# A dense expert layer whose second product keeps its sums in PSUM, tokens in rows, the second table streamed past loaded weights

## The chip, the cores and the metric

One core of one Trainium2 chip runs the whole program. The metric is the device time of one execution in microseconds (us); the median of three timed runs stands for a kernel.

## What is computed

Two transformer blocks follow each other on 512 tokens of 1024 values, in 32-bit floats. The change touches the end of the second block, a layer of 16384 small experts of which each token uses 8 times 16, and the final norm:

```python
q = (hc @ w_query).reshape(TOKEN_CHUNK, PEER_HEADS, 2, PEER_HALF)
...
gate = jax.nn.softmax(top_s, axis=-1)
u = expert_u[expert_idx]
act = jax.nn.gelu(jnp.einsum('thkd,td->thk', u, hc).astype(jnp.float32), approximate=False)
vv = expert_v[expert_idx]
return jnp.einsum('thk,thkd->td', (gate * act).astype(hc.dtype), vv)
...
x = x + peer_ffn(h2, ...)
return rmsnorm_2(x, final_g)
```

## The kernel before

Most tokens are computed densely. The first DT = 416 tokens are multiplied with all of both tables, in 128 tiles of 128 experts each. For a tile of the first table (a **U part**) the sum over the 1024 values of h gives one number per expert and token; GELU and the gate (zero for experts that the token did not choose) turn it into a weight; a tile of the second table (a **V part**) is multiplied with these weights and added to x. The other 96 tokens (3 sets of 32) go **by rows**: GpSimd gathers, for 32 tokens and four groups of experts at a time, 128 table rows (512 KB), and DVE reduces them against h (first 96 steps, line 1710) or adds them up with their weights (last 96 steps, lines 1720 and 1723), one step per gather.

A 32-bit product is made of three on TensorE: every operand is split into a high part and a remainder, and `mm3` multiplies high by high, high by remainder and remainder by high. The tables arrive as raw tiles of 512 KB (`stream`, slots of a ring of 4: SP loads `raw`, ACT makes `hi`, POOL makes `lo` on line 600). h is `inH`, `inL`; weights are `WH`, `WL`. x is kept transposed, as `xT`: 8 pieces k of 128 values, tokens along the row.

In a **U part** the table is the loaded operand and 416 tokens are streamed: 8 values of k by three products, 24 products. In a **V part** the table is the loaded operand too, and 416 columns of weights are streamed: for each of the 8 pieces k of x a pair of tiles gives 6 products in bank k mod 4, and DVE adds that bank to `xT` (`add`, line 1701). TensorE waits (`y_added`) until the bank is free again. A pair of tiles so has 48 products in its V parts and 8 additions on DVE.

The order is written out per engine. 48 U parts are computed before the loop: 20 while DVE looks for the chosen experts, 24 between the batches in which DVE builds the gates as one-hot products (`onehots`, 52 batches of 8 tokens, lines 1666 to 1670), and 4 behind them; 16 of their results are spilled to memory. The expert loop goes by pairs: 8 pairs with V parts alone (`HEAD`), 40 with U parts 32 tiles ahead and V parts, 16 with V parts alone. On ACT each pair has the copies of the stored results (line 1017), the high parts of the weights (1022) and of the tables (1041, 1108), and the GELU (1052); on DVE the gating (1692), the remainders (1697), the additions and the steps of the rows. For each set TensorE turns h (`turn_h`) and later the sums of the set (`turn_acc`). At the end the final norm needs all of x: squares, a sum over partitions on TensorE, a root, and the scaling of 8 pieces (1783) with one output transfer each.

## Time and profile before

| what | us |
| --- | --- |
| median of 3 timed runs | 2474.28 (2474.09 to 2475.71) |
| the profiled execution, its own time | 2468.48 |
| its span in the profile | 2466.7 |
| first product of the expert loop starts | 1496.80 |
| last product of the expert loop starts | 2453.59 |

The profile is a page with busy time by engine, by slices and by groups of instructions, and a trace that can be asked for a stretch. PE is TensorE's products, PEld its weight loads, DVE, ACT and POOL the other engines, SP issues transfers. A product's record is longer than the distance to the next one, because products overlap: the distance of two starts is what a product costs.

### The profile page before, as it was taken

The numbers are of one execution on the slowest core, as the hardware profiler recorded it, in microseconds if no ns is written. First come the engines' busy times: TensorE is split into PE (matmuls) and PEld (weight loads), VectorE is DVE, ScalarE is ACT, GpSimd is POOL, SyncE is SP. The second block draws the span as 40 slices with busy tenths as digits, with TensorE's granted clock in tenths as the row PEclk, the third lists the DMA queues.
The fourth block names the chain that finished last, engine by engine and source line by source line (L and its number), as shares of the span: only waits on it lengthen the run. The fifth ranks groups of instructions, "written<-read, shape, count | busy, mean of one in ns | idle before, by whom it ended". The sixth has DMA issues, their size and how long they took to land.

```text
span 2466.7 us, 37389 instructions
## 1 busy us (share of the span) xinstructions
PE 2404.9 (97%) x13120; PEld 2160.3 (88%) x13120; DVE 1685.8 (68%) x3413; ACT 929.9 (38%) x1473; POOL 1329.5 (54%) x1183
## 2 busy tenths in 40 slices
PE   7999999999999999999998999999999999999998
PEld 6785788888888886778998899899999999999998
DVE  6476733332499977779999985866766667575566
ACT  3146122222322346514354554333333343434443
POOL 5520565656555662364410006777777777776553
PEclk9999999999999999999999999999999999999999
DMA  4210233223232222132225678978888888786453
GB/s 171 94 52 27 77 102 102 94 100 105 85 111 94 95 85 82 49 105 86 90 90 185 249 267 277 344 257 279 266 276 270 270 277 272 256 299 208 144 169 100
DMA packets 211993, 404.48 MB, mean 164 GB/s; under 512 B 118432, under 2 KB 124960, under 8 KB 208544
## 3 DMA queue, kind: packets, MB, share of 16 engines
q1 hardware_dynamic: 64224, 233.36, 28.8%
q0 software_dynamic: 27648, 100.68, 10.9%
q10 hardware_dynamic: 120000, 68.89, 9.4%
q8 instruction: 69, 1.13, 0.2%
q14 instruction: 52, 0.43, 0.1%
HBM read 370.10 MB, written 32.77 MB: 163 GB/s over the span
## 4 chain that ended last, share of the span: by engine, by line
PE 72%; DVE 19%; issue 4%; POOL 3%; ACT 1%; DMA 0%; ACTq 0%; DVEq 0%; POOLq 0%; SPq 0%
PE bank L1790 22%; PE bank L1792 22%; PE bank L1791 22%; POOL lo L600 3%; DVE ohg L1670 2%; DVE lo L1609 2%; DVE oh L1666 1%; PE bank L1948 1%; DVE oh L1667 1%; PE bank L1959 1%; PE bank L1935 1%; DVE rows L1710 1%; DVE idx L1568 1%; DVE idx L1560 1%; DVE scb L1561 1%
## 5 line engine op out<-in xcount | busy, mean ns | idle before, releaser
L600 POOL TENSOR_TENSOR lo<-raw,hi 128x256 fp32r<-128x256 f32 (+1 forms) x948 | 1131.0, 1223 | 994.3 <-ACT hi L686 559.9
L1790 PE MATMUL bank<-inH,hi 128*128 128x512 f32 (+1 forms) x2112 | 790.5, 374 | 18.0 <-DVE inL L1137 13.4
L1792 PE MATMUL bank<-inH,lo 128*128 128x512 f32 (+1 forms) x2112 | 781.7, 370 | 0.0
L1791 PE MATMUL bank<-inL,hi 128*128 128x512 f32 (+1 forms) x2112 | 781.5, 370 | 0.0
L1790 PEld LDWEIGHTS bank<-inH,hi 128*128 128x128 f32 x2112 | 396.7, 188 | 67.2 <-POOL lo L600 12.8
L1792 PEld LDWEIGHTS bank<-inH,lo 128*128 128x128 f32 x2112 | 396.6, 188 | 43.5
L1791 PEld LDWEIGHTS bank<-inL,hi 128*128 128x128 f32 x2112 | 397.2, 188 | 42.0 <-issue 0.2
L1701 DVE TENSOR_TENSOR xT<-xT,bank 128x416 f32<-128x416 f32 x504 | 286.7, 583 | 213.3 <-PE bank L1792 108.5
L686 ACT ACTIVATE hi<-raw 128x1024 fp32r<-128x1024 f32 x236 | 247.9, 1056 | 405.0 <-PE bank L1792 392.2
L1790 PE MATMUL bank<-WH,hi 128*128 128x416 f32 x1024 | 358.9, 350 | 8.0 <-DVE xT L1701 7.2
L1791 PE MATMUL bank<-WL,hi 128*128 128x416 f32 x1024 | 357.7, 349 | 0.0
L1792 PE MATMUL bank<-WH,lo 128*128 128x416 f32 x1024 | 357.4, 349 | 0.0
L1041 ACT ACTIVATE hi<-raw 128x1024 fp32r<-128x1024 f32 x176 | 179.8, 1047 | 208.0 <-PE bank L1792 199.7
L1790 PEld LDWEIGHTS bank<-WH,hi 128*128 128x128 f32 x1024 | 192.5, 188 | 11.0 <-DVE xT L1701 9.0
L1792 PEld LDWEIGHTS bank<-WH,lo 128*128 128x128 f32 x1024 | 192.7, 188 | 0.3
L1791 PEld LDWEIGHTS bank<-WL,hi 128*128 128x128 f32 x1024 | 192.6, 188 | 0.3
L1692 DVE TENSOR_TENSOR bank<-bank,Gd 128x416 f32<-128x416 f32 x128 | 76.0, 595 | 114.1 <-ACT bank L1017 97.2
L1487 DVE SCALAR_TENSOR_TENSOR bank<-u,gn,bank 128x512 f32<-128x512 f32 x224 | 148.2, 750 | 0.0
L1723 DVE SCALAR_TENSOR_TENSOR bank<-rows,gate_sp,bank 128x1024 f32<-128x1024 f32 x93 | 119.4, 1284 | 1.3
L1710 DVE CUSTOM_DVE_ANT_0 rows<-bank,rows 128x1024 f32<-128x1024 f32 x96 | 116.0, 1218 | 0.0
L1052 ACT ACTIVATE A<-bank 128x416 f32<-128x416 f32 x80 | 41.5, 519 | 193.7 <-PE bank L1792 191.2
L1022 ACT ACTIVATE WH<-bank 128x416 fp32r<-128x416 f32 x128 | 65.6, 513 | 120.5 <-DVE bank L1692 98.1
(325 smaller groups left out, 2920.8 us busy)
## 6 DMA issues: line engine op xcount, KB each, us to landing
raw<-stream SPq DMA_DIRECT2D x440, 512.0 KB
Gd<-gates ACTq DMA_DIRECT2D x32, 832.0 KB
gates<-stage_a ACTq DMA_DIRECT2D x13, 1024.0 KB, 4.8
gates<-stage_b ACTq DMA_DIRECT2D x13, 1024.0 KB, 4.1
A<-spilled ACTq DMA_DIRECT2D x8, 416.0 KB
tbl<-gqa ACTq DMA_DIRECT2D x8, 384.0 KB, 3.2
xT<-x SPq DMA_DIRECT2D x4, 512.0 KB, 7.8
out<-xT ACTq DMA_DIRECT2D x8, 256.0 KB, 2.0
```

The lines of the kernel that those rows point to most:

```text
L600: ins = pool.tensor_tensor(lo[:, r, part], raw[:, r, part], hi[:, r, part].bitcast(F32), ALU.subtract)
L686: act.activation(hi[:, r % RING, :], raw[:, r % RING, :], ACT.Copy).then_inc(hi_done, 1)
L1022: act.activation(WH[:, j % 2, e, :DT], staged(j, e), ACT.Copy).then_inc(high_w, 1)
L1041: act.activation(hi[:, r, :], raw[:, r, :], ACT.Copy).then_inc(hi_done, 1)
L1487: done.append(chain.mark(dve.scalar_tensor_tensor(to, *tap(j), d, ALU.mult, ALU.add)))
L1692: dve.tensor_tensor(a, a, Gd[:, buf, :, 2 * (j % 2) + e, :], ALU.mult).then_inc(gate_done, 1)
L1701: dve.tensor_tensor(xT[:, k, :DT], xT[:, k, :DT], B[k % 4][:, :DT], ALU.add).then_inc(y_added, 1)
L1710: dve.tensor_tensor_reduce(out=rows[r][:, :], in0=held, in1=rows[r][:, :], scale=1.0, scalar=0.0, op0=ALU.mult, op1=ALU.add, accum_out=dot ...
L1723: dve.scalar_tensor_tensor(held, rows[r][:, :], weight, held, ALU.mult, ALU.add).then_inc(row_used, 1)
L1790: pe.matmul(bank, wh, xh, start=start, stop=False)
L1791: pe.matmul(bank, wh, xl, start=False, stop=False)
L1792: return pe.matmul(bank, wl, xh, start=False, stop=stop_)
```

## The change

- 128 tokens go by rows instead of 96 (4 sets), so DT is 384 (three blocks of 128); 256 steps and gathers instead of 192. h for them is turned once, before the loop, and copied into four groups by transfers on ACT's queue (`spread_h`).
- In a V part the **weights** are the loaded operand and the table is streamed: for each block of 128 tokens three products by two halves of 512 columns, 18 products in all. They add to six PSUM banks (three blocks by 1024 values) over all 128 tiles; x is turned into those banks first (`turn_x`), and there is no addition on DVE and no `y_added`.
- The loop goes by single tiles: 47 with a V part alone, then 80 turns of a U part (tile t+1) and a V part (tile t), then the last V part. Weights have 4 buffers.
- The remainders of the tables are made by POOL for odd slots and by DVE for even ones.
- One more U part (21) comes ahead of the batches and one fewer (23) between them; there are 48 batches instead of 52.
- The steps are dealt out by `steps_of`: a tile with a V part alone counts 3, another 8. Gathers are issued one tile ahead, into 6 buffers.
- The final norm goes by token: ACT squares a block's 1024 values and adds them up, DVE scales (`scale_block`); the output is stored by blocks, the rows' block ahead of the loop's end.

```diff
-SET, SETS = 32, 3
+SET, SETS = 32, 4
 DT = T - SET * SETS
+DB = DT // P
 GROUPS = P // SET
-PHASE_PAIRS = (5, 5, 5, 5, 4, 4, 4)
-FIRST_PAIR = 4
-ROWS_AHEAD = 5
+ROWS_AHEAD = 6
...
-EARLY = 19
+EARLY = 20
...
+FIRST_STEPS, LAST_STEPS = 4, 122
+PHASES = ((FIRST_STEPS, 75), (78, LAST_STEPS))
...
+def v_slot(t):
+    return t if t < V_ONLY else min(V_ONLY + 2 * (t - V_ONLY) + 1, N_REST - 1)
...
+    return sum(3 if at < V_ONLY else 8 for at in range(first, t + 1))
...
+def steps_of(t):
+    for phase, (first, last) in enumerate(PHASES):
+        if first <= t <= last:
+            n, whole = N_STEPS // 2, share(first, last)
+            return range(phase * n + n * share(first, t - 1) // whole, phase * n + n * share(first, t) // whole)
...
+            with sp.Fori(1, N_REST // RING) as i:
+                for r in range(RING):
+                    sp.wait_ge((lo_even, lo_odd)[r % 2], i * 2 + (r // 2 - 1))
+                    load(i * RING + (S_REST + r), r)
...
+            def odd_low(i):
...
+                if i % 2 == 0:
+                    return
+                n, r = S_REST + i, i % RING
+                pool.wait_ge(hi_done, n + 1)
+                pool.tensor_tensor(lo[:, r, :], raw[:, r, :], hi[:, r, :].bitcast(F32), ALU.subtract).then_inc(lo_odd, 1)
...
+            for t in range(NKEY):
+                if t + 3 <= V_ONLY:
+                    odd_low(t + 3)
+                elif V_ONLY <= t + 1 and t + 3 < NKEY:
+                    odd_low(u_slot(t + 3))
...
+                for g in steps_of(t + 1):
+                    gather(g)
...
+            def high_rest(i):
+                if i < N_REST:
+                    act.wait_ge(loaded[i % RING], 16 * ((S_REST + i) // RING + 1))
+                    act.activation(hi[:, i % RING, :], raw[:, i % RING, :], ACT.Copy).then_inc(hi_done, 1)
...
+            def spread_h(of):
...
+                act.wait_ge(row_used, SET * (of - 1)) if of >= 2 else act.wait_ge(x_turned, TT)
+                act.wait_ge(h_out, 2)
+                for grp in range(GROUPS):
+                    act.dma_start(h_rep[of % 2][grp * SET:(grp + 1) * SET, :],
+                                  h_tok[of * SET:(of + 1) * SET, :]).then_inc(h_in[of % 2], 16)
...
+            for t in range(NKEY - 1):
...
+                if t + 1 < N_EARLY:
+                    if t:
+                        move(t + 1)
+                else:
+                    act.wait_ge(slot_used, S_PEER + t + 2)
+                    act.activation(staged(t + 1), staged(t + 1), ACT.Gelu).then_inc(a_moved, 1)
+                    high_rest(u_slot(t + 1) + RING)
+                if t:
+                    high_w_part(t + 1)
...
+                act.wait_ge(y_done, t + 1)
+                high_rest(v_slot(t) + RING)
+                sparse_out(t)
+            for b in range(DB):
+                act.wait_ge(block_done, b + 1)
+                block_out(b, banks[:, 2 * b:2 * b + 2, :].rearrange("p b t -> p (b t)"), b + 1)
...
-            def add(j, k):
-                dve.wait_ge(y_done, j * KD + (k + 1))
-                dve.tensor_tensor(xT[:, k, :DT], xT[:, k, :DT], B[k % 4][:, :DT], ALU.add).then_inc(y_added, 1)
...
+            def even_low(i):
...
+                if i % 2:
+                    return
+                n, r = S_REST + i, i % RING
+                dve.wait_ge(hi_done, n + 1)
+                dve.tensor_tensor(lo[:, r, :], raw[:, r, :], hi[:, r, :].bitcast(F32), ALU.subtract).then_inc(lo_even, 1)
...
+                if of < SETS:
...
+                        dve.wait_ge(h_in[of % 2], 16 * GROUPS * (of // 2 + 1))
...
+            for t in range(NKEY - 1):
+                steps = list(steps_of(t))
+                if t + 3 <= V_ONLY:
+                    even_low(t + 3)
+                elif V_ONLY <= t + 1 < NKEY - 1:
+                    even_low(v_slot(t + 1))
+                for g in steps[:len(steps) // 2]:
                     step(g)
-                if j == V_PAIRS:
-                    fold_in(SETS - 1)
-            for e in (0, 1):
...
+                if t:
+                    gated(t + 1)
+                    low_part(t + 1)
+                for g in steps[len(steps) // 2:]:
+                    step(g)
...
+            dve.wait_ge(gain_in, 16)
+            scale_block(TT - 1, lambda half: x_sp[:, half * T:(half + 1) * T], 0)
+            for b in range(DB):
+                scale_block(b, lambda half: B[2 * b + half][:, :], b + 1)
...
+            def turn_x(b, at):
...
+                for k in range(KD):
+                    m = pe.matmul(B[at + k // 4][:, k % 4 * P:(k % 4 + 1) * P], xT[:, k, b * P:(b + 1) * P], ident, start=k % 4 == 0, stop=k % 4 == 3 and b == TT - 1)
+                m.then_inc(x_turned, 1)
...
-            def mix(j, wpar, n_lo, r):
...
-                pe.wait_ge(lo_done, n_lo)
-                pe.wait_ge(w_done, j * 2 + 2)
+            def expert_u(t, i, e, r):
+                pe.wait_ge(w_done, t - 1)
+                pe.wait_ge((lo_even, lo_odd)[r % 2], i)
                 for k in range(KD):
-                    if not isinstance(j, int) or j * KD + k - 3 > 0:
-                        pe.wait_ge(y_added, j * KD + (k - 3))
                     c = slice(k * P, (k + 1) * P)
-                    for e in (0, 1):
-                        m = mm3(B[k % 4][:, :DT], hi[:, r + e, c], lo[:, r + e, c], WH[:, wpar, e, :DT], WL[:, wpar, e, :DT],
-                                e == 0, e == 1)
+                    m = mm3(B[6 + e][:, :DT], hi[:, r, c], lo[:, r, c], inH[:, k, :DT], inL[:, k, :DT], k == 0, k == KD - 1)
+                m.then_inc(slot_used, 1)
+            def expert_v(t, i, w, r, stop=False):
+                pe.wait_ge(w_done, t + 1)
+                pe.wait_ge((lo_even, lo_odd)[r % 2], i)
+                for b in range(DB):
+                    tok = slice(b * P, (b + 1) * P)
+                    for x, table in ((WH, hi), (WH, lo), (WL, hi)):
+                        for half in (0, 1):
+                            last = x is WL
+                            m = pe.matmul(B[2 * b + half], x[:, w, tok], table[:, r, half * T:(half + 1) * T], start=False, stop=stop and last)
+                    if stop:
+                        m.then_inc(block_done, 1)
+                if not stop:
                     m.then_inc(y_done, 1)
...
+            pe.wait_ge(w_done, 2)
+            turn_x(0, 0)
+            with pe.Fori(0, V_ONLY // 4) as i:
+                for c in range(4):
+                    expert_v(i * 4 + c, i * 2 + (c // 2 + 1), c, c)
+            for t in range(V_ONLY // 4 * 4, V_ONLY):
+                expert_v(t, t // 2 + 1, t % W_TILES, t % RING)
+            with pe.Fori(0, (NKEY - N_EARLY) // 4) as i:
+                for c in range(4):
+                    t, at = V_ONLY + c, V_ONLY + 2 * c
+                    expert_u(i * 4 + (t + 1), i * 4 + (at // 2 + 1), (t + 1) % 2, at % RING)
+                    expert_v(i * 4 + t, i * 4 + ((at + 1) // 2 + 1), t % W_TILES, (at + 1) % RING)
+            expert_v(NKEY - 1, (N_REST - 1) // 2 + 1, (NKEY - 1) % W_TILES, (N_REST - 1) % RING, stop=True)
```

On TensorE, in the joint part of the loop, before: the end of a U part and the start of a V part (WH and WL are streamed, hi and lo loaded; `bank` is a PSUM bank).

```order
L1792 MATMUL bank<-inH,lo 128x416
L1790 MATMUL bank<-WH,hi 128x416 [waits y_added,w_done,lo_done]
L1791 MATMUL bank<-WL,hi 128x416
L1792 MATMUL bank<-WH,lo 128x416
L1790 MATMUL bank<-WH,hi 128x416
L1791 MATMUL bank<-WL,hi 128x416
L1792 MATMUL bank<-WH,lo 128x416
L1790 MATMUL bank<-WH,hi 128x416 [waits y_added]
```

And now: the end of a V part and the start of the next U part; rows with x2 are two products.

```order
L2373 REGISTER_ALU [waits w_done]
L2379 MATMUL bank<-hi,WH 128x512 [waits lo_even]
L2379 MATMUL bank<-hi,WH 128x512
L2379 MATMUL bank<-lo,WH 128x512 x2
L2379 MATMUL bank<-hi,WL 128x512 x2
L2379 MATMUL bank<-hi,WH 128x512 x2
L2379 MATMUL bank<-lo,WH 128x512 x2
L2379 MATMUL bank<-hi,WL 128x512 x2
L2379 MATMUL bank<-hi,WH 128x512 x2
L2379 MATMUL bank<-lo,WH 128x512 x2
L2379 MATMUL bank<-hi,WL 128x512 x2
L1840 MATMUL bank<-inH,hi 128x384 [waits lo_odd,w_done]
```

The table is now what is streamed, in 512 columns, two products for each loaded block, and nothing waits for an addition.

On DVE, in the first part of the loop (V parts alone), before: one pair with the first of its five steps (L1710).

```order
L1692 TENSOR_TENSOR bank<-bank,Gd 128x416 [waits a_moved,g_loaded0]
L1701 TENSOR_TENSOR xT<-xT,bank 128x416 [waits y_done] x2
L1697 TENSOR_TENSOR WL<-bank,WH 128x416 [waits high_w]
L1692 TENSOR_TENSOR bank<-bank,Gd 128x416 [waits a_moved,g_loaded0]
L1701 TENSOR_TENSOR xT<-xT,bank 128x416 [waits y_done] x2
L1697 TENSOR_TENSOR WL<-bank,WH 128x416 [waits high_w]
L1701 TENSOR_TENSOR xT<-xT,bank 128x416 [waits y_done]
L1710 ISA rows_126,dots<-bank,rows_126 128x1024 [waits h_turned,row_in0]
L1710 ISA dots 128x1
L1701 TENSOR_TENSOR xT<-xT,bank 128x416 [waits y_done]
L1710 ISA rows_127,dots<-bank,rows_127 128x1024 [waits row_in1]
L1710 ISA dots 128x1
```

And now: the weights of tiles 6 and 7 and the start of tile 8 (L1784 is a step, L1775 the remainder of a table tile).

```order
L1775 TENSOR_TENSOR lo<-raw,hi 128x1024 [waits hi_done]
L1762 TENSOR_TENSOR bank<-bank,Gd 128x384 [waits a_moved,g_loaded1]
L1767 TENSOR_TENSOR WL<-bank,WH 128x384 [waits high_w]
L1784 ISA rows_130,dots<-h_rep_136,rows_130 128x1024 [waits row_in1]
L1784 ISA dots 128x1
L1762 TENSOR_TENSOR bank<-bank,Gd 128x384 [waits a_moved,g_loaded1]
L1767 TENSOR_TENSOR WL<-bank,WH 128x384 [waits high_w]
L1784 ISA rows_134,dots<-h_rep_136,rows_134 128x1024 [waits row_in2]
L1784 ISA dots 128x1
L1775 TENSOR_TENSOR lo<-raw,hi 128x1024 [waits hi_done]
L1762 TENSOR_TENSOR bank<-bank,Gd 128x384 [waits a_moved,g_loaded0]
L1767 TENSOR_TENSOR WL<-bank,WH 128x384 [waits high_w]
```

The additions are gone; each second tile has a remainder that stands ahead of the gating, and one step follows each tile's weights.

On POOL, in the first part of the loop, before: the five gathers for a pair behind two remainders.

```order
L600 TENSOR_TENSOR lo<-raw,hi 128x1024 [waits hi_done] x2
L655 DMA rows_126<-rows_u,expert 128x1024 [waits row_used]
L655 DMA rows_127<-rows_u,expert 128x1024 [waits row_used]
L655 DMA rows_128<-rows_u,expert 128x1024 [waits row_used]
L655 DMA rows_129<-rows_u,expert 128x1024 [waits row_used]
L655 DMA rows_131<-rows_u,expert 128x1024 [waits row_used]
L600 TENSOR_TENSOR lo<-raw,hi 128x1024 [waits hi_done] x2
```

And now, one remainder and the gathers of two tiles in turn.

```order
L715 TENSOR_TENSOR lo<-raw,hi 128x1024 [waits hi_done]
L706 DMA rows_139<-rows_u,expert 128x1024
L706 DMA rows_129<-rows_u,expert 128x1024 [waits row_used]
L715 TENSOR_TENSOR lo<-raw,hi 128x1024 [waits hi_done]
L706 DMA rows_130<-rows_u,expert 128x1024 [waits row_used]
L706 DMA rows_134<-rows_u,expert 128x1024 [waits row_used]
L715 TENSOR_TENSOR lo<-raw,hi 128x1024 [waits hi_done]
L706 DMA rows_135<-rows_u,expert 128x1024 [waits row_used]
L706 DMA rows_138<-rows_u,expert 128x1024 [waits row_used]
```

A gather was issued a pair ahead of its use, behind the remainders of the pair before; it is now issued one tile ahead.

## Rows read from the trace of the kernel before

**Rows 1.** The page, section 1: busy time of each engine, share of the span, instructions.
```profile
PE 2404.9 (97%) x13120; PEld 2160.3 (88%) x13120; DVE 1685.8 (68%) x3413; ACT 929.9 (38%) x1473; POOL 1329.5 (54%) x1183
```

**Rows 2.** Stretches of the expert loop: busy time of each engine, clock, DMA.
```profile
core 0: us, PE busy (x) PEld busy (x) DVE busy (x) ACT busy (x) POOL busy (x), PEclk, DMA share, GB/s
1545.00:1580.00 35.00, 29.94 (x142) 27.84 (x141) 35.00 (x67) 11.78 (x18) 28.63 (x22) 0.93 1.03 384
1590.00:2300.00 710.00, 710.00 (x3836) 709.78 (x3835) 457.93 (x717) 275.93 (x399) 533.71 (x325) 1.00 0.79 263
```

**Rows 3.** Timeline, PE: start, duration; end of a V part, start of a U part.
```profile
2200.92 0.35 PE L1792 MATMUL bank<-WH,lo 128*128 128x416 f32 x1
2201.11 0.35 PE L1790 MATMUL bank<-inH,hi 128*128 128x416 f32 x1
2201.30 0.35 PE L1791 MATMUL bank<-inL,hi 128*128 128x416 f32 x1
```

**Rows 4.** Timeline, PE, 512 columns: the first and the last of eleven.
```profile
699.73 0.39 PE L1791 MATMUL bank<-inL,hi 128*128 128x512 f32 x1
...
701.99 0.39 PE L1792 MATMUL bank<-inH,lo 128*128 128x512 f32 x1
```

**Rows 5.** Timeline, PEld, 256 columns: the first and the last of seven weight loads.
```profile
122.51 0.19 PEld L1791 LDWEIGHTS bank<-lo,inH 128*128 128x128 f32 x1
...
123.22 0.19 PEld L1791 LDWEIGHTS bank<-lo,inH 128*128 128x128 f32 x1
```

**Rows 6.** Timeline, ACT: the first GELU of two pairs that follow each other.
```profile
1662.83 0.52 ACT L1052 ACTIVATE A<-bank 128x416 f32<-128x416 f32 x1 [2.47 <-PE bank L1792]
...
1680.75 0.52 ACT L1052 ACTIVATE A<-bank 128x416 f32<-128x416 f32 x1 [2.47 <-PE bank L1792]
```

**Rows 7.** Timeline, PE: the first and the last product of the expert loop.
```profile
1496.80 0.43 PE L1790 MATMUL bank<-WH,hi 128*128 128x416 f32 x1 [0.16 <-DVE WL L1697]
...
2453.59 0.34 PE L1792 MATMUL bank<-WH,lo 128*128 128x416 f32 x1
```

**Rows 8.** Groups by shape: busy us, mean ns, then idle before it.
```profile
L600 POOL TENSOR_TENSOR lo<-raw,hi 128x1024 fp32r<-128x1024 f32 x228 | 548.5, 2428 | 492.2 <-DVEq L1672 222.0 <-ACT hi L1041 153.4 <-ACT hi L1108 58.3
...
L1701 DVE TENSOR_TENSOR xT<-xT,bank 128x416 f32<-128x416 f32 x504 | 286.7, 583 | 213.3 <-PE bank L1792 108.5 <-issue 104.0
...
L1710 DVE CUSTOM_DVE_ANT_0 rows<-bank,rows 128x1024 f32<-128x1024 f32 x96 | 116.0, 1218 | 0.0
L655 POOL DMA_INDIRECT rows<-rows_u,expert x96 | 91.4, 952 | 30.8 <-issue 22.9 <-DVE dots L1710 6.4
...
L1609 DVE TENSOR_TENSOR lo<-raw,hi 128x1024 fp32r<-128x1024 f32 x32 | 39.2, 1225 | 5.5 <-DVE ohg L1670 5.1
```

**Rows 9.** Timeline, ACT, pairs with V work alone: one turn.
```profile
2321.48 0.94 ACT L1017 ACTIVATE bank<-A 128x416 f32<-128x416 f32 x2
2322.72 0.52 ACT L1022 ACTIVATE WH<-bank 128x416 fp32r<-128x416 f32 x1 [0.30 <-DVE bank L1692]
```

**Rows 10.** Timeline, POOL and DVE: the fifth gather and the step that uses it.
```profile
1528.65 0.94 POOL L655 DMA_INDIRECT rows<-rows_u,expert  x1 [0.30 <-issue]
...
1540.29 1.22 DVE L1710 CUSTOM_DVE_ANT_0 rows<-bank,rows 128x1024 f32<-128x1024 f32 x1
```

**Rows 11.** The page, section 6: issue to landing in us (last number).
```profile
tbl<-gqa ACTq DMA_DIRECT2D x8, 384.0 KB, 3.2
xT<-x SPq DMA_DIRECT2D x4, 512.0 KB, 7.8
```

**Rows 12.** Timeline, DVE, building of gates: the start of two batches.
```profile
1334.81 0.69 DVE L1666 TENSOR_TENSOR oh<-i1T,iota 128x1024 f16<-128x1024 f16 x1
...
1337.44 0.69 DVE L1666 TENSOR_TENSOR oh<-i1T,iota 128x1024 f16<-128x1024 f16 x1
```

**Rows 13.** Timeline, PE: half of one turn of 128 by 1024 values.
```profile
1525.75 1.05 PE L2318 MATMUL bank<-cs,res 128*128 128x128 f32 x8
```

**Rows 14.** Timeline, DVE: the last eight operations.
```profile
2458.87 5.35 DVE L1783 SCALAR_TENSOR_TENSOR xT<-xT,gn,bank 128x512 f32<-128x512 f32 x8 [1.25 <-PE bank L1879]
```

478 lines of the change are left out of this document (200 added, 278 removed).

## Prediction

> **What bounds the kernel now.** I first read the busy times: PE is busy for 97% of the span, DVE for 68%, POOL for 54% [rows 1]. PE's share counts records that overlap, so I went on to distances of starts. In the expert loop, between 1590 and 2300 us, PE is busy for all of the 710 us and DVE for 458 [rows 2], and a pair of tiles takes 1680.75 - 1662.83 = 17.92 us [rows 6]. A pair has 96 products, so one costs 17.92 / 96 = 0.1867 us, which is what neighbouring starts show (0.19, the bank changing between the first two without a gap) [rows 3]. The loop is bound by the number and width of products, and by nothing else there. From first to last product it takes 2453.9 - 1496.8 = 957.1 us [rows 7]. The products alone would need 24 pairs x 8.96 + 40 x 17.92 = 931.8 us; the other 25 are turns, waits near the start, where DVE is busy without a pause (35.00 of 35 us) and a moment at half clock (0.93 in those 35 us) [rows 2].
>
> **What a product costs at the new widths.** Ten distances at 512 columns take 701.99 - 699.73 = 2.26 us, 0.226 each [rows 4]. At 256 columns six take 123.22 - 122.51 = 0.71 us, 0.118 each [rows 5]. Between 256 and 416 columns the slope is 0.00043 us a column, between 416 and 512 it is 0.00041: a straight line. For 384 columns it gives 0.1867 - 32 x 0.00043 = 0.173 us. A U part goes from 24 x 0.1867 = 4.48 to 24 x 0.173 = 4.15 us, a V part from 4.48 to 18 x 0.226 = 4.07 us.
>
> The weight loads are busy for 709.78 of 710 us in the loop [rows 2], each 0.19 us long, as long as the distance of two products. At 256 columns they are still 0.19 long and start 0.118 apart [rows 5], so one load can run into the next, and I take the straight line. The Trainium skill (Perfetto Trace Analysis, Identifying the Most-Contended Engine) tells to judge the headroom of TensorE by the busy share of weight loads; by that this loop has none, and a narrower stream would bring nothing. That is rival B.
>
> **The loop, if PE is never held up:** 47 x 4.07 + 80 x (4.15 + 4.07) + 4.07 = 853.0 us, 104.1 less than now.
>
> **What the other engines need per turn.** In a joint turn of 8.22 us DVE has a gating and a remainder of weights (each like the 0.58 us of line 1701, an operation of that size), a table remainder of 1.225, and 128 / 45 = 2.84 steps of 1.22: 5.9 us. POOL has one remainder of 2.43 and 2.84 gathers, each 0.95 and about 0.3 between: 6.0 us [rows 8]. The additions that fell away were 8 x 0.58 us a pair on DVE. Both fit. The weights of tile t+1 have from the end of their U part until the next V part but one, 8.2 us, for a chain of less than 4. I expect no wait there.
>
> With V parts alone a turn is only 4.07 us, and three things show. (a) **The start:** ACT has two sets of h to send out, 8 issues of about 0.4 us, ahead of tile 2's weights: 4 us once (an estimate). (b) **The chain through ACT and DVE.** After a V part ends, ACT makes the high part of a table tile (1.0), DVE for each second tile its remainder (1.15 before it is free again), then gating 0.56, high weights 0.5, remainder of weights 0.56, with 0.1 to 0.3 us at each hand-over [rows 8, 9]. Sum about 4.35 us against 4.07: 0.3 us for each second tile, 22 x 0.3 = 7 us. Without the remainder the chain takes 3.6 and is hidden. (c) **The gathers.** A gather is now issued one tile ahead. From the end of V part t-1: 1.2 us to ACT's high part, 2.5 for POOL's remainder, then the gather at +3.9; it lands L later; the step takes 1.2, the next weights 1.9; V part t+3 is due at +12.2. There is room for L = 5.2 us. Every us above that delays one V part in four, about 10 us over the 42 tiles. L itself no row shows: before, a gather was issued 1540.29 - 1528.65 = 11.6 us ahead of its use and DVE never waited [rows 10]. The nearest rows are two other transfers, 3.2 us for 384 KB in a quiet place and 7.8 for 512 KB in a crowd [rows 11]. I take 6, somewhat above the middle, because the memory queues are full here: 8 us. The ends are 0 and 26. Together 4 + 7 + 8 = 19 us, and I keep 2.5 us for half clock (35 x 0.07), since PE again has small pauses: 874.5 us, **82.6 less**.
>
> **Ahead of the loop.** The building of gates is set by DVE: a batch takes 1337.44 - 1334.81 = 2.63 us [rows 12], 4 fewer batches save 10.5. The extra small copies for the fourth set I leave out. PE's narrower U parts save nothing there as DVE is later. `turn_h` and the turns of x between the batches lie in PE's slack (23 x 4.15 us of U parts is 12 less than 24 x 4.48); the last turn comes after the first weights: half a turn is 0.9 to 1.05 us [rows 13], so 1.8. DVE's first weights go one tile after the other, 0.5 more. Net **8.2 less**. If the weights are not what comes last here, it is between 4 and 10.
>
> **The end.** From the last product to the end of the span there are 2466.7 - 2453.9 = 12.8 us now; the last scaling ends at 2458.87 + 5.35 = 2464.2, 2.5 us before the end [rows 14]. After the change three blocks follow each other at 1.36 us; ACT needs about 1.6 for each (a pass over 1024 values like the 1.04 of the table's high part, and a root), DVE 1.6 (two scalings of 0.67, a reciprocal): ACT ends 2.1 us after the last product, DVE 2.6 later, and 2.5 for the store: 7.2. **5.6 less**, with the rows' block stored earlier. An end of 5 or 10 us is possible.
>
> **Sum:** 82.6 + 8.2 + 5.6 = 96.4 us less. The profiled span is 2466.7, its own time 2468.48; the median of the runs is 5.8 us above that, and I take the difference from the median: 2474.28 - 96.4 = 2378 us.
>
> **Rivals.**
>
> A. *The gathers are late.* For it: DMA demand in the first part is (2.06 x 0.524 + 0.197) MB in 4.07 us, 314 GB/s, and 361 while the spilled results come back; the trace shows 384 over 35 us at a share of 1.03 [rows 2]. So the queues stand full, and 7.8 us or more per gather is no wonder. With 7.8 the time is 18 us more, 2396; with 10 us 2418; I take 2407. Against: as the loop slows the demand falls.
>
> B. *Weight loads bind U parts.* Their 24 loads of 0.187 keep 4.48 us: 128 x 0.33 = 42 us lost, 2420. Rows 5 speak against it.
>
> C. *DMA can't feed the joint turns, and the kernel is slower.* A turn needs (4.84 x 0.524 + 0.197) = 2.73 MB in 8.22 us, 333 GB/s, for 80 turns. Before it was 263 GB/s at a busy share of 0.79 [rows 2]; 263 / 0.79 is 333, so if a byte keeps its cost there is nothing to spare. Against: the 384 GB/s. If the flow stops at 280 GB/s, a turn takes 9.76, 80 x 1.54 = 123 us more: 2501. It ends slower than before below about 291 GB/s (a turn of 9.4 us).
>
> D. *The accumulation costs more than the sum says.* Each product now goes to another bank than the last one; before the bank changed each 6 products in a V part, without a gap [rows 3]. If each of the 2304 cost 0.05 us more, it would be 115 us: 2493, slower. From 0.042 it eats the gain.
>
> **Chances.** The forecast 0.60, A 0.16, B 0.06, C 0.07, D 0.03; 0.08 for what I have not seen (0.04 of it for a larger gain, with no wait in the first part and a shorter end, 0.02 for no change, 0.02 for slower). The range from 2355 (no waits at all in the loop, a shorter end) to 2425 (the ends of the gathers' price, and B) holds the forecast, nearly all of A, and B. A measurement of this kernel can tell 0.2% from no change, some 5 us: faster 0.86, same 0.02, slower 0.12.
>
> **What would show it.** Starts of 384-column products 0.173 apart and of 512-column ones 0.226; U parts of the joint turns 8.22 us apart, with PE busy throughout and no wait named. In the first part, PE's waits on the remainder of weights, of a few tenths each second tile, and some on DVE steps that wait for their rows; first part near 210 us instead of 191. The loop should start about 8 us earlier, near 1488, and the end should take 7 us. If the turns are longer with DVE or POOL waiting for transfers, C is right; if PE is busy but the starts are further apart, B or D.

## The result, and the profile after

| | before | after |
| --- | --- | --- |
| median of the timed runs, us | 2474.72 (2474.09 to 2475.71) | 2448.03 (2441.85 to 2453.88) |
| ratio, 95% interval | | 0.9891 (0.9864 to 0.9919) |
| span of the profiled execution | 2466.7 | 2442.9 |
| first product of the loop | 1496.80 | 1491.85 |
| loop, first to last product | 957.1 | 945.1 |
| from there to the end of the span | 12.8 | 6.0 |

The kernel is faster by 26.7 us, 1.1%. The forecast was 96 us, and the time lies outside its range. The spans of the profiled executions differ by 23.8 us where 96.4 were forecast; of the missing 72.6 us, 70.6 are in the loop (945.1 for 874.5).

Section 1 of the page after, which answers [rows 1]: every engine but DVE has less to do.

```profile
PE 2342.1 (96%) x12272; PEld 1990.8 (81%) x12272; DVE 1734.1 (71%) x3084; ACT 872.5 (36%) x1386; POOL 1269.1 (52%) x1143
```

Stretches of the loop after, which answer [rows 2]. The first goes to the start of the 48th V part (46 turns with a V part alone and one joint turn), the second to the end; "first part" and "joint part" mean these two below, the joint part without the last V part of 4.1 us.

```profile
core 0: us, PE busy (x) PEld busy (x) DVE busy (x) ACT busy (x) POOL busy (x), PEclk, DMA share, GB/s
1491.85:1747.77 255.92, 218.54 (x874) 172.09 (x872) 145.91 (x207) 89.84 (x140) 129.81 (x72) 0.93 0.77 249
1747.77:2436.90 689.13, 674.42 (x3355) 605.92 (x3354) 556.86 (x543) 232.12 (x328) 488.81 (x288) 0.99 0.87 305
```

Without waits the forecast had 46 x 4.07 + 8.22 = 195.4 us for the first part; it took 255.9, at a granted clock of 0.93. The joint part has 79 x 8.22 + 4.07 = 653.4 against 685.0. What PE waited for, in the first part and after it (us in sum, times, longest):

```profile
PE bank L2379 <- DVE WL L1767: 37.3, 13, 5.2
...
PE bank L2379 <- DVE WL L1767: 13.7, 12, 5.2
```

The products themselves cost what was forecast, as the timeline of PE shows in the joint part, a U part between two V parts (it answers [rows 3, 4]; "x2" is two products):

```profile
1950.28 0.62 PE L2379 MATMUL bank<-hi,WL 128*128 128x512 f32 x2
1950.74 0.33 PE L1840 MATMUL bank<-inH,hi 128*128 128x384 f32 x1
...
1954.92 0.63 PE L2379 MATMUL bank<-hi,WH 128*128 128x512 f32 x2
...
1959.04 0.33 PE L1840 MATMUL bank<-inH,hi 128*128 128x384 f32 x1
```

The U part takes 1954.92 - 1950.74 = 4.18 us (forecast 4.15), the V part 4.12 (4.07). A turn is 8.30 to 8.31 instead of 8.22.

The groups by shape on DVE and POOL from 1485 on (busy us, mean ns, idle before and what ended it), which answer [rows 8]:

```profile
L1775 DVE TENSOR_TENSOR lo<-raw,hi 128x1024 fp32r<-128x1024 f32 x104 | 192.7, 1854 | 33.2 <-ACT hi L1120 33.0
L1795 DVE SCALAR_TENSOR_TENSOR acc<-rows,gate_sp,acc 128x1024 f32<-128x1024 f32 x124 | 192.6, 1553 | 29.7 <-DMA rows<-rows_v,expert 25.8 <-issue 0.3 <-DVE acc L1795 0.2
L1784 DVE CUSTOM_DVE_ANT_0 rows<-h_rep,rows 128x1024 f32<-128x1024 f32 x128 | 192.3, 1515 | 56.3 <-DMA rows<-rows_u,expert 54.7 <-issue 1.2
...
L715 POOL TENSOR_TENSOR lo<-raw,hi 128x1024 fp32r<-128x1024 f32 x104 | 284.1, 2732 | 259.7 <-ACT hi L1120 248.6 <-ACT hi L749 10.7 <-issue 0.2
L706 POOL DMA_INDIRECT rows<-rows_u,expert x128 | 172.2, 1345 | 32.3 <-issue 26.0 <-DVE dots L1784 1.8
```

DVE's steps, alone 1.22 us as in [rows 8], have a mean of 1.51 and 1.55; its remainder of a table tile, 1.225 before, has 1.85. POOL's remainder went from 2.43 to 2.73, its gather from 0.95 to 1.35. And DVE waits for its rows, 85 us in sum, which it never did before.

The timeline round one wait in the first part, POOL, then DVE, then PE:

```profile
1617.07 2.41 POOL L715 TENSOR_TENSOR lo<-raw,hi 128x1024 fp32r<-128x1024 f32 x1 [5.76 <-ACT hi L1120]
1619.62 1.77 POOL L706 DMA_INDIRECT rows<-rows_u,expert  x1
...
1625.49 2.39 POOL L715 TENSOR_TENSOR lo<-raw,hi 128x1024 fp32r<-128x1024 f32 x1 [2.09 <-ACT hi L1120]
...
1626.07 2.90 DVE L1784 CUSTOM_DVE_ANT_0 rows<-h_rep,rows 128x1024 f32<-128x1024 f32 x1 [1.88 <-DMA rows<-rows_u,expert]
...
1630.01 0.56 DVE L1767 TENSOR_TENSOR WL<-bank,WH 128x384 fp32r<-128x384 f32 x1 [0.56 <-ACT WH L1096]
...
1628.08 0.61 PE L2379 MATMUL bank<-hi,WL 128*128 128x512 f32 x2
1630.62 0.82 PE L2379 MATMUL bank<-hi,WH 128*128 128x512 f32 x2 [1.93 <-DVE WL L1767]
1631.24 1.05 PE L2379 MATMUL bank<-lo,WH 128*128 128x512 f32 x2
```

It reads from the top. POOL makes a remainder and issues the gather at 1619.62. DVE has waited 1.88 us for those rows when its step starts at 1626.07, 6.45 us after the issue. POOL has begun its next remainder at 1625.49, which ends at 1627.88; the step ends 1.09 us behind that, so it takes 2.90 instead of 1.22. The gating and the weights follow, and PE has waited 1.93 us. Then the products are slow for some 3 us: two cost 0.86 us (1631.24 on), at a granted clock of 0.50, that is 1.2 GHz, where 0.45 is usual. From 1551 us on PE waits like this about every 20 us, in every fourth or fifth turn.

The 1.09 us are no accident. In this trace 91 operations of DVE with two operands in SBUF (steps and table remainders) began while POOL was inside a remainder. Each of them ended 1.08 to 1.13 us behind the end of that POOL instruction, whenever it had begun, and so took 1.28 to 3.43 us; the 185 that met no remainder took 1.21 to 1.33. It goes the other way too: 69 remainders of POOL began inside such an operation of DVE, and all ended 2.23 to 2.26 us behind its end. And all 107 gathers that took more than 1.3 us on POOL ended 0.81 to 0.84 us behind such an operation of DVE. So the two engines don't share at a lower speed; the one that comes second does nothing until the other's instruction is over.

The timeline of ACT shows a third thing: two places where issues of transfers hold it for 10 us. In the first the first of the four issues takes 8.11 us and the others 0.61 each; the second is one issue.

```profile
1811.92 0.37 ACTq L1078 DMA_DIRECT2D Gd<-gates  x1
1812.47 10.05 ACTq L1127 DMA_DIRECT2D h_rep<-h_tok  x4
...
2121.81 0.37 ACTq L1078 DMA_DIRECT2D Gd<-gates  x1
2122.30 9.56 ACTq L1154 DMA_DIRECT2D gain_row<-last_gain  x1
```

Behind them stand the longest turns of the joint part: 10.88 and 12.03, 13.71 and 11.26 us.

### The profile page after: what moved, and what is told of

It is laid out like the page before. It is cut to its first block, busy times and chain, and to the rows that moved or that the text cites. A ratio compares the mean times of both kernels' runs of the same rounds, so it can differ in the third digit from the quotient of the medians.

```text
span 2442.9 us, 34890 instructions
## 1 busy us (share of the span) xinstructions
PE 2342.1 (96%) x12272; PEld 1990.8 (81%) x12272; DVE 1734.1 (71%) x3084; ACT 872.5 (36%) x1386; POOL 1269.1 (52%) x1143
## 4 chain that ended last, share of the span: by engine, by line
PE 54%; DVE 19%; issue 8%; DMA 8%; POOL 7%; ACT 3%; ACTq 1%; DVEq 0%; POOLq 0%; SPq 0%
PE bank L1840 13%; PE bank L1842 13%; PE bank L1841 13%; PE bank L2379 9%; DMA rows<-rows_u,expert 4%; DMA rows<-rows_v,expert 3%; POOL lo L651 3%; POOL lo L715 3%; DVE acc L1795 3%; DVE ohg L1740 2%; ACT hi L1120 1%; PE bank L1998 1%; DVE lo L1679 1%; PE bank L2009 1%; PE bank L1985 1%
## 5 line engine op out<-in xcount | busy, mean ns | idle before, releaser
L651 POOL TENSOR_TENSOR lo<-raw,hi 128x256 fp32r<-128x256 f32 (+1 forms) x740 | 631.7, 885 | 770.4 <-ACT hi L749 551.8
L1840 PEld LDWEIGHTS bank<-inH,hi 128*128 128x128 f32 x2112 | 398.4, 189 | 80.8 <-issue 16.7
L715 POOL TENSOR_TENSOR lo<-raw,hi 128x1024 fp32r<-128x1024 f32 x104 | 284.1, 2732 | 259.7 <-ACT hi L1120 248.6
L2379 PE MATMUL bank<-hi,WH 128*128 128x512 f32 x768 | 251.1, 409 | 52.1 <-DVE WL L1767 51.0
L2379 PE MATMUL bank<-lo,WH 128*128 128x512 f32 x768 | 245.3, 401 | 0.0
L2379 PE MATMUL bank<-hi,WL 128*128 128x512 f32 x768 | 243.0, 398 | 0.0
L1784 DVE CUSTOM_DVE_ANT_0 rows<-h_rep,rows 128x1024 f32<-128x1024 f32 x128 | 192.3, 1515 | 56.3 <-DMA rows<-rows_u,expert 54.7
L1775 DVE TENSOR_TENSOR lo<-raw,hi 128x1024 fp32r<-128x1024 f32 x104 | 192.7, 1854 | 33.2 <-ACT hi L1120 33.0
L1795 DVE SCALAR_TENSOR_TENSOR acc<-rows,gate_sp,acc 128x1024 f32<-128x1024 f32 x124 | 192.6, 1553 | 29.7 <-DMA rows<-rows_v,expert 25.8
L706 POOL DMA_INDIRECT rows<-rows_u,expert x128 | 172.2, 1345 | 32.3 <-issue 26.0
L706 POOL DMA_INDIRECT rows<-rows_v,expert x128 | 164.7, 1287 | 32.1 <-issue 28.5
```

The source lines that it names most:

```text
L651: ins = pool.tensor_tensor(lo[:, r, part], raw[:, r, part], hi[:, r, part].bitcast(F32), ALU.subtract)
L706: pool.indirect_dma_start(rows[r][:, :], None, table, bass.IndirectOffsetOnAxis(expert[:, column:column + 1], 0)).then_inc(row_in[r], 16)
L715: pool.tensor_tensor(lo[:, r, :], raw[:, r, :], hi[:, r, :].bitcast(F32), ALU.subtract).then_inc(lo_odd, 1)
L1775: dve.tensor_tensor(lo[:, r, :], raw[:, r, :], hi[:, r, :].bitcast(F32), ALU.subtract).then_inc(lo_even, 1)
L1784: dve.tensor_tensor_reduce(out=rows[r][:, :], in0=h_rep[of % 2][:, :], in1=rows[r][:, :], scale=1.0, scalar=0.0, op0=ALU.mult, op1=ALU.add ...
L1795: dve.scalar_tensor_tensor(total[:, :], rows[r][:, :], weight, total[:, :], ALU.mult, ALU.add).then_inc(row_used, 1)
```

## The experiments

Causes thought of at first: theory 1, DVE and POOL slow each other down; 2, the gathers land late; 3, the chain of ACT and DVE with ACT's transfers; 4, the products are slower than forecast. All times of parts come from the starts of V parts in the profiled run; the median and the ratio to the kernel before from 4 or 5 timed runs. The kernel before, timed with each group of them, had medians of 2473.5 to 2477.4, so the ratio compares two rows better than the medians do.

| kernel | median | ratio | first part | joint part |
| --- | --- | --- | --- | --- |
| after | 2448.0 | 0.9891 | 255.9 | 685.0 |
| e1_neither | 2373.5 | 0.9581 | 210.0 | 660.3 |
| e2_steps_no_gathers | 2391.4 | 0.9650 | 222.1 | 664.5 |
| e3_gathers_short_steps | 2400.2 | 0.9695 | 230.9 | 665.3 |
| e4_pool_low_cut | 2397.4 | 0.9690 | 227.5 | 663.6 |
| e5_issues_on_sync | 2424.9 | 0.9797 | 245.2 | 674.2 |
| e6_gathers_ahead | 2407.5 | 0.9736 | 216.1 | 683.5 |
| e7_weights_first | 2446.1 | 0.9889 | 251.5 | 687.7 |
| e8_pool_lows_first_part | 2455.8 | 0.9924 | 262.2 | 686.8 |
| e9_sync_and_ahead | 2388.2 | 0.9655 | 211.0 | 671.7 |
| e10_sync_ahead_weights | 2378.0 | 0.9612 | 201.5 | 669.5 |
| e11_step_between | 2381.7 | 0.9631 | 202.8 | 673.9 |
| e12_both_pool_low_cut | 2371.5 | 0.9595 | 205.5 | 660.3 |
| e13_away_from_gates | 2421.8 | 0.9795 | 249.8 | 669.5 |
| e14_low_behind_in_joint | 2389.4 | 0.9664 | 200.5 | 681.6 |
| e15_gates_on_sync | 2431.5 | 0.9833 | 245.6 | 672.4 |
| e16_pool_low_pieces | 2392.3 | 0.9679 | 205.9 | 680.5 |

### What is the floor, and which part of the rows' work costs

**e1_neither**: gathers of g % 128 < 6 alone, and

```diff
-dve.tensor_tensor_reduce(out=rows[r][:, :], in0=h_rep[of % 2][:, :], ...
+dve.tensor_tensor_reduce(out=rows[r][:, :16], in0=h_rep[of % 2][:, :16], ...
-dve.scalar_tensor_tensor(total[:, :], rows[r][:, :], weight, total[:, :], ...
+dve.scalar_tensor_tensor(total[:, :16], rows[r][:, :16], weight, total[:, :16], ...
```

> Left out: the work of the 128 tokens by rows in the loop. All gathers but the first six of either table are gone, and each of the 256 steps on DVE is cut to 16 columns (with a small factor, so that the numbers stay finite). What is left is the dense loop with its chain ACT - DVE. After the change the loop takes 945 us, forecast were 874.5 with 853.0 for PE alone. Theory 1 (stretched operations: DVE and POOL slow each other when both read SBUF, steps of 1.22 us take up to 3.4): the loop falls to 857 to 865 us and the time to about 2365. Theory 2 (the gathers land late): the same, this run does not tell the two apart. Theory 3 (the chain ACT - DVE and the transfers at the ends of sets cost most): the first 47 tiles still take over 230 us (now 256), the loop over 900. Theory 4 (products in V parts really cost 0.230 instead of 0.226): joint turns stay at 8.31 us and the loop is not under 865.

Stretches of e1_neither, the same two parts and columns:

```profile
1495.62:1705.65 210.03, 204.05 (x873) 162.46 (x872) 89.90 (x209) 91.04 (x140) 63.36 (x30) 0.99 0.68 207
1705.65:2370.10 664.45, 664.45 (x3355) 604.05 (x3354) 329.94 (x541) 232.54 (x328) 197.21 (x85) 1.00 0.52 154
```

The dense loop takes 874.5 us, by chance the number forecast for the whole. The joint part is at 660.3, all turns 8.31; the first part has two turns of 8.59 and 5.82 us at the start (ACT sends out h) and then nearly all of 4.25 and 4.21 in turn. So theory 4 holds with 660.3 - 653.4 = 6.9 us, and theory 3 falls as far as it is about the chain. Its other half, ACT's transfers, this run can't judge: in its loop no issue held ACT for more than 1.75 us. The rows' work costs 70 us of the loop although PE does none of it.

**e2_steps_no_gathers** has the gathers cut as in e1, the steps whole. **e3_gathers_short_steps** has all gathers, the steps cut.

> Left out: the gathers of all steps but the first six of either table; DVE does all 256 steps in full, on what stands in the buffers, and waits for no transfer. Theory 1 (operations of DVE stretched by POOL's work): the steps are still stretched where POOL makes its remainders (mean near 1450 ns instead of 1515), and the loop is at 885 to 910 us. Theory 2 (late gathers): nothing is late, the loop falls to 860 to 870 us, within 8 us of the run without steps and gathers. If neither, and the loop stays above 920, DVE's place in the chain is what costs.

> Left out: nearly all of the steps' arithmetic. All gathers are made and waited for as now, but each step is 16 columns wide, so DVE is free 1.2 to 3.4 us earlier for each. Theory 1 (stretched operations): most of the 70 us come back, the loop is at 865 to 880 us. Theory 2 (late gathers): a row that is late holds DVE as long as now less the 1.2 us of the step itself, so the waits for rows on DVE (now 80 us in sum) stay over 40 us and the loop over 890 us.

The loop of e2 took 890.8 us, which is in the range of theory 1, the loop of e3 900.2 us, which is in the range of theory 2: neither alone is the cause. Steps without gathers keep 12 of the 46 us of the first part, gathers with short steps 21, though DVE then waited 326 us in sum for rows. In e2 DVE's steps were stretched to means of 1.60 and 1.75 us by POOL's remainders, and little waited for them. It takes a late row and a long step together. e3 also tells how DVE is slowed: its steps of 16 columns take 0.16 to 0.23 us alone, but 81 that began inside a remainder of POOL took up to 2.34 us and ended 0.03 to 0.04 us behind it.

**e4_pool_low_cut**:

```diff
-pool.tensor_tensor(lo[:, r, :], raw[:, r, :], hi[:, r, :] ...
+pool.tensor_tensor(lo[:, r, :16], raw[:, r, :16], hi[:, r, :16] ...
```

> Left out: most of POOL's remainders of the odd table tiles in the loop (16 of 1024 columns are made). Everything else is as in the changed kernel; the gathers that stand behind them on POOL go out up to 2.7 us earlier. Theory 1 (DVE and POOL slow each other): DVE's steps and remainders are no longer stretched, mean 1220 to 1300 ns against 1515 and 1854 now, POOL's gathers go back from 1.3 to 0.95 us, and the loop gains 40 us or more (under 905). Theory 2 (late gathers): the means of DVE's operations stay where they are, over 1450, and the loop gains by the earlier issue alone, 10 to 30 us.

Groups of DVE in e4_pool_low_cut:

```profile
L1795 DVE SCALAR_TENSOR_TENSOR acc<-rows,gate_sp,acc 128x1024 f32<-128x1024 f32 x124 | 159.0, 1282 | 83.0 <-DMA rows<-rows_v,expert 80.2
L1784 DVE CUSTOM_DVE_ANT_0 rows<-h_rep,rows 128x1024 f32<-128x1024 f32 x128 | 155.5, 1222 | 63.9 <-DMA rows<-rows_u,expert 63.6
L1775 DVE TENSOR_TENSOR lo<-raw,hi 128x1024 fp32r<-128x1024 f32 x104 | 127.0, 1222 | 56.8 <-ACT hi L1120 56.4
```

All three are back to what they take alone, 1.28, 1.22 and 1.22 us: the stretching comes with POOL's remainder. The loop gained 50 us, but here the gathers also go out 2.4 us earlier, and in the first part DVE's waits for rows fell from 26.7 to 7.1 us, so it doesn't say which of the two it was.

### One cause at a time, with nothing left out

**e6_gathers_ahead**: POOL asks for gathers up to six steps ahead of DVE, as many as there are buffers.

```diff
-                for g in steps_of(t + 1):
-                    gather(g)
+                while t + 1 >= FIRST_STEPS and asked < min(N_STEPS, max(end(t + 1), end(t - 1) + ROWS_AHEAD)):
+                    gather(asked)
+                    asked += 1
```

> Nothing is left out: a gather is issued as soon as its buffer can be free by the order of DVE (six steps ahead) instead of one tile ahead, that is up to four gathers earlier in the first part, the same in joint turns. Theory 2 (late gathers): DVE's waits for rows_u in the first part (26.7 us in 13) nearly vanish and the first 47 tiles fall from 256 to about 225 us, the time to about 2418. Theory 1 alone (stretched operations set the pace, whatever the lead): DVE waits less for rows, but its stretched operations stay, and the first part gains under 8 us.

Stretches of e6_gathers_ahead:

```profile
1493.14:1709.27 216.13, 205.28 (x873) 163.54 (x872) 139.06 (x209) 90.54 (x140) 135.93 (x74) 0.98 0.92 304
1709.27:2396.90 687.63, 673.66 (x3355) 605.88 (x3354) 561.77 (x541) 232.66 (x328) 484.59 (x285) 0.99 0.87 302
```

This was the largest cause: the first part fell by 39.8 us. By the waits of PE 26.3 of them are waits (37.3 to 11.0), and by the granted clock 13.6 are half clock (0.07 x 255.9 to 0.02 x 216.1); PE's busy time, 218.5 to 205.3, says the same. DVE's steps are no shorter (1.58 and 1.59 us) and it waits for no row in the first part; with rows in time hardly anything waits for long steps there. The joint part, where the lead is the same, kept its 683.5.

**e5_issues_on_sync**: SP issues h, the spilled results, the gain row and the sums.

```diff
-                    act.dma_start(gain_row[:, :], last_gain).then_inc(gain_in, 16)
...
+                    sp.dma_start(gain_row[:, :], last_gain).then_inc(gain_in, 16)
```

> Nothing is left out: the transfers of the loop that ACT issues (h for the sets, the spilled results, the sums of the sets, the gain row; all but the gates) are issued by SP between its table tiles. In the changed kernel ACT was held by such issues for 10.05, 9.56, 8.30, 5.20 and 4.46 us, and PE's longest waits follow them. Theory H (held issues): the two pairs of long turns in the joint part (10.88 and 12.03, 13.71 and 11.26 us) go back to 8.3 and the long ones at the start of the loop shrink, 20 to 30 us in all, the time near 2420. Rival (the issues only stand where DVE and the gathers are late anyway, or SP's table tiles get late behind them): under 8 us, 2440 to 2450.

The gain is 23 us, half in either part: theory H holds. On SP none of these issues took more than 1.16 us.

**e7_weights_first** moves DVE's `even_low(t + 3)` behind `low_part(t + 1)` in the first part; **e8_pool_lows_first_part** gives all remainders of the first part to POOL.

> Nothing is left out: in the first part of the loop DVE makes the remainder of a table tile (needed three turns later) behind the gating and the remainder of the next weights instead of ahead of them. Theory (the remainder stands in the chain of the weights, 1.2 us alone and 3.4 us where POOL holds it up): turns without a hold-up go from 4.25 and 4.21 in turn to 4.08, 7 us, and the 6.3 us turns shrink, 10 to 20 us more; the first part from 256 to 230 to 240 us, the time about 2425 to 2430. Rival (DVE is late for its rows, not for its remainders): the first part gains 7 us at most, and a remainder made later may hold up the table tiles.

> Nothing is left out: in the first part of the loop POOL makes all remainders of the tables, the even ones too, as it did before the change; the joint part is as in the changed kernel. DVE has 1.2 us less to do in each second tile, POOL 2.4 us more. Theory 1 (DVE and POOL slow each other, and the gathers stand behind POOL's remainders): the steps are stretched more often, the gathers land later, and the first part takes 256 us or more, the time 2445 to 2475. Rival (DVE's place in the chain is what costs, and taking work from it helps): the first part falls to about 240 us, the time to about 2432.

e7 brought 2 us, within the spread of the runs: its free turns took 4.08 us as expected, but the turns with a late row got longer (6.47 instead of 6.30). The theory named the wrong link. e8 lost 8 us, 6.3 of them in the first part: POOL's longer work sends the gathers later, and DVE's waits for rows there went from 26.7 to 41.0 us. Both speak for late rows.

### Together

**e9_sync_and_ahead** is e5 and e6; **e10_sync_ahead_weights** adds e7.

> Nothing is left out: the transfers of ACT moved to SP (gain alone: 23 us, 11 of them in the joint part) and the gathers asked for six steps ahead (gain alone: 41 us, nearly all in the first part). If the two causes are different ones, the gains add up but for what they share at the start of the loop (some 8 us): first part about 206 us, joint part about 674, the time near 2392. If both only remove the same waits: not under 2403.

> Nothing is left out: as the run with both (transfers on SP, gathers ahead), and in the first part DVE makes a table remainder behind the next weights. Alone this order gained nothing that counts (2 us), since the rows were late; its turns without a wait took 4.08 us instead of 4.23 on average. With the rows in time it should now show: 47 x 0.15 = 7 us, first part about 198 us, the time near 2385. If the remainder, made later, holds up the table tiles, nothing is gained against 2392.

Both medians came out better than expected, by 4 and 7 us, though the first parts are 5.0 and 3.5 us longer. So the two causes are different ones. e7, worth nothing alone, now gains 10 us. Stretches of e10_sync_ahead_weights:

```profile
1491.91:1693.45 201.54, 196.98 (x873) 162.87 (x872) 143.95 (x209) 90.17 (x140) 128.49 (x74) 1.00 0.98 327
1693.45:2367.10 673.65, 669.45 (x3355) 602.92 (x3354) 562.35 (x541) 232.70 (x328) 487.50 (x285) 1.00 0.89 308
```

Its 2378 us (ratio 0.9612, 0.9597 to 0.9628) are 70 us less than the changed kernel, with the same computation. That this is the number of the forecast is chance: its first part and its joint part miss theirs by -15 and +16 us.

**e12_both_pool_low_cut** is e9 with POOL's remainders cut as in e4.

> Left out: most of POOL's remainders of the odd table tiles in the loop (16 of 1024 columns are made); else as the run with transfers on SP and gathers ahead. It measures what the slowing of DVE by POOL's remainders costs once the late gathers and the held issues are gone. Theory 1 as it now stands (it costs in joint turns, where DVE has little to spare): joint part from 674 to 661 to 665 us, the first part 3 us at most, the time 10 to 14 us under the run with both. If stretched operations no longer matter: less than 4 us.

```profile
1491.59:1697.04 205.45, 202.32 (x873) 161.37 (x872) 131.66 (x209) 90.14 (x140) 55.67 (x74) 1.00 0.97 322
1697.04:2361.50 664.46, 664.46 (x3355) 604.10 (x3354) 440.15 (x541) 235.37 (x328) 251.12 (x285) 1.00 0.89 312
```

The joint part is at the floor, 660.3. With e9 at 671.7, the slowing of DVE by POOL's remainders costs 11.4 us there. It isn't that the rows come earlier: in the joint part of e12 DVE waited 87 us for rows, in e9 49, and PE waited for nothing. The first part fell by 5.5 us, all at one place near its start (turns of 8.90 and 5.82 us became 5.01 and 4.20). These are single profiled runs; the medians are 16.7 apart.

The long joint turns of e9 and e10 take 8.70 us. One of them in e10, POOL's remainder and then DVE:

```profile
2096.22 2.94 POOL L754 TENSOR_TENSOR lo<-raw,hi 128x1024 fp32r<-128x1024 f32 x1 [1.35 <-ACT hi L1162]
...
2096.82 3.42 DVE L1804 TENSOR_TENSOR lo<-raw,hi 128x1024 fp32r<-128x1024 f32 x1
...
2102.48 0.56 DVE L1796 TENSOR_TENSOR WL<-bank,WH 128x384 fp32r<-128x384 f32 x1 [0.56 <-ACT WH L1138]
...
2105.53 3.42 DVE L1804 TENSOR_TENSOR lo<-raw,hi 128x1024 fp32r<-128x1024 f32 x1
```

From one table remainder to the next DVE has 8.71 us of work, with no gap but the one for ACT's high part; with 1.22 us for the remainder it would be 6.5.

**e11_step_between**, **e14_low_behind_in_joint** and **e16_pool_low_pieces** tried to win these 11 us from e10: a step put into DVE's wait for the high part; the table remainder put behind the weights; POOL's remainder in four instructions.

```diff
-                pool.tensor_tensor(lo[:, r, :], raw[:, r, :], hi[:, r, :] ...
+                for c in range(0, D, T // 2):
+                    part = slice(c, c + T // 2)
+                    ins = pool.tensor_tensor(lo[:, r, part], raw[:, r, part], hi[:, r, part] ...
```

> Nothing is left out: as the run before in this list, and in the joint turns DVE does one step between the gating and the remainder of the weights, where it now waits 0.56 us for ACT's high part (124 times, 73 us in sum). Where turns take 8.70 us (some 30 of 80) DVE has no idle time left but this; with 0.56 us less they should go to 8.31: 10 us less, the joint part about 664 us, the time near 2375. Rival (the 8.7 us are set by POOL's remainder and gathers, which DVE only waits for): joint turns stay at 8.7, under 3 us gained.

> Nothing is left out: the fastest version so far (transfers on SP, gathers ahead, in the first part the table remainder behind the weights: 2377.95), and in joint turns too DVE makes the table remainder behind the weights. Its start then no longer coincides with POOL's remainder, which follows the same high parts of ACT: the mean of DVE's table remainders falls from 1747 to under 1500 ns and most joint turns of 8.7 go to 8.31, up to 8 us gained, near 2371. Rival (the sum of shared time decides, not the order): other operations are stretched instead, the time stays within 3 us of 2378, or is longer since the remainder is now the last thing that the V part waits for.

> Nothing is left out: the fastest version so far, with POOL's remainder of a table tile made in four instructions of 256 columns instead of one of 1024. Theory L (whichever of the two has begun keeps the other out for its whole instruction): the longest of DVE's table remainders falls from 3.41 to about 2 us and the means of its steps from about 1580 to 1400 ns or less, while POOL's remainder gets longer (four starts, some 3.2 instead of 2.7 us); joint turns of 8.7 us get fewer, 0 to 8 us gained. Rival (both are slowed in proportion while they overlap): the longest remainder stays above 3 us.

All three lost, 4, 11 and 14 us. In e11 and e16 DVE is quicker and then waits for rows (127 and 139 us in sum, e10 45), since in joint turns the gathers go out no earlier; in e14 PE waits for the table remainder itself (10.8 us). e16 still tells what it was made for. DVE's remainder (shortest, median, longest ns) and POOL's:

```profile
L1807 DVE TENSOR_TENSOR lo<-raw,hi x104: 1211/1219/1764, 1491.7 to 2364.7; 128x1024 fp32r<-128x1024 f32 x104
...
L756 POOL TENSOR_TENSOR lo<-raw,hi 128x256 fp32r<-128x256 f32 x416 | 411.0, 1019 | 125.6 <-ACT hi L1165 114.0 <-ACT hi L794 10.3 <-issue 0.3
```

The longest of DVE's remainders is 1.76 us instead of 3.42. What holds DVE up is one POOL instruction, whole, and the rival, a slowing in proportion, falls. But POOL's four now take 4 x 1.02 = 4.1 us instead of 2.7, so it is no cure.

### Why an issue holds ACT

Either the gathers' traffic or the gates' load ahead of it on ACT's queue, 768 KB in pieces of 256 B. **e13_away_from_gates** issues the same transfers one or two turns later where they stood behind that load; **e15_gates_on_sync** moves the gates' loads to SP.

```diff
+            set_ends = {t + (2 if t % 4 == 2 else 1 if t % 4 == 3 else 0): of for t, of in set_ends.items()}
...
-                if t % 2 and t < N_SPILLED:
+                s = t if t % 4 == 1 else t - 1 if t and t % 4 == 0 else N_SPILLED
+                if s < N_SPILLED:
```

> Nothing is left out: the changed kernel, with ACT's transfers (spilled results, h, gain row, sums) issued one or two turns later wherever they stood right behind a load of the gates (768 KB in pieces of 256 B, every fourth tile, on the same queue); the gathers and all else are as they were. Theory G (the queue is full of the gates' pieces, and the next issue waits until it drains): the issues of 4.46, 8.30, 10.05 and 9.56 us fall to under 1.5 us for one transfer, the joint part from 685 to about 672 us, the first part by 5 to 10 us; time about 2426 to 2430. Rival (the gathers' traffic holds them): some issues still take 4 us and more, and less than 5 us are gained.

> Nothing is left out: the changed kernel, with the gates' loads of the loop issued by SP between its table tiles, and all other transfers still by ACT. Theory G: ACT's issues are short again (h and gain row under 3 us in sum of four), and the hold moves to SP: single table tiles behind a gates' load are issued 4 to 10 us late and land late, so the gain is anywhere between 25 us and a loss. Rival (gathers): ACT's issues of h and the gain row still take 9 us and more.

ACT in e13_away_from_gates, the same two transfers:

```profile
1824.39 0.54 ACTq L1127 DMA_DIRECT2D h_rep<-h_tok  x1
...
1824.96 1.96 ACTq L1127 DMA_DIRECT2D h_rep<-h_tok  x3
...
2124.36 0.35 ACTq L1155 DMA_DIRECT2D gain_row<-last_gain  x1
```

10.05 us became 2.50 for four issues, and 9.56 became 0.35; one issue of 3.55 us is left. The median fell by 26 us, the joint part by 15.5. e15 shows that the hold goes with the gates' load: SP is held at the next table tile behind it, and ACT is free.

```profile
2104.62 0.38 SPq L635 DMA_DIRECT2D Gd<-gates  x1
2108.06 9.75 SPq L613 DMA_DIRECT2D raw<-stream  x1
...
2104.72 0.35 ACTq L1163 DMA_DIRECT2D gain_row<-last_gain  x1
```

In e15 an issue of a table tile took more than 1 us behind most loads of the gates; in the changed kernel, with the same loads on ACT's queue, none of SP's took more than 0.45. So it is the order on the queue. Behind the load issued at 1811.92 in the changed kernel one can see it drain: its 3072 pieces start between 1814.1 and 1824.6 us, and the issue behind it was over at 1820.6, when four fifths of them had started. The gathers are not needed for it: without them (e2) such issues took 4.63 and 8.38 us. But in e1, without gathers and long steps, none took more than 1.75, and what sets the length stays open.

## Why the prediction failed, step by step

- **Cost of products**: right. 4.18 and 4.12 us for 4.15 and 4.07; over the joint part 6.9 us. Rivals B and D fall. The Trainium skill (Perfetto Trace Analysis, Identifying the Most-Contended Engine) names the busy share of weight loads beside the share of peak arithmetic; read as in rival B it would have kept 4.48 us for a U part, and the trace, with 4.18, doesn't agree with that.
- **DMA in joint turns (C)**: right that it holds. e12 makes all transfers, at 312 GB/s, and every turn takes 8.31 us.
- **Start (a) and chain (b)**: 4 + 7 us and 2.5 for half clock were forecast; e1, which has only these, has 210.0 - 195.4 = 14.6 us. Right in size; the 8 issues took 5.2 us for 4, and the chain costs some 0.15 us in each turn instead of 0.3 in each second.
- **The gathers (c)** is the step that failed. They were priced at 8 us; e6, which takes the lateness away, gives back 39.8 us in the first part. The latency is the smaller part of the error: in the 13 places of the first part where DVE waited, the step began 6.4 to 7.8 us after the issue of its gather, median 6.55, and I took 6. At my own 10 us for each us above 5.2 that is 14 us. The error is the price of a late row, which I took to be only what exceeds 5.2 us. The traces show that a late row meets POOL's next remainder: in 8 of the 13 places the step took 2.1 to 3.0 us instead of 1.22. And after 8 of its 13 waits PE ran at half clock for 3 to 6 us. After five others, of 1.9 to 2.6 us, it didn't; why, no run shows.
- **Rival A** names the gathers too, but with 7.8 us or more for each, and 2396 to 2418 us. The first part had less than that, and the time lies outside: its name came true, not its mechanism.
- **"I expect no wait" in joint turns**: wrong. The need of DVE, 5.9 us, was summed with 1.22 us a step, from rows of a kernel in which DVE's steps had one operand in PSUM (`held`) and its table remainders ran while POOL had no remainders to make. The change took h and the sums of the rows to SBUF, and I didn't see that it puts both operands there. With 3.42 us for a table remainder the need is 8.7 us in the worst turns, and that costs 11.4 us (e9 and e12). The rule was to be had. The Trainium skill (SBUF — State Buffer, Who interferes with whom) says that a DVE instruction with two inputs in SBUF contends with a GpSimd instruction that reads SBUF, and that the port they share is an exclusive lock. The traces agree, with 91 of 91 operations that waited for the end of POOL's instruction. The rule spoke against this part of the change, and it isn't in my list of rivals.
- **ACT's issues at 0.4 us**: wrong, and put at nothing outside the start: 10.7 us in the first part and 10.8 in the joint part by e5. The trace of before had the sign. Its rows of DVE and ACT ahead of the loop:

```profile
1473.12 1.29 DVE L1670 TENSOR_TENSOR ohg<-oh,gpart 128x1024 f16<-128x1024 f16 x2
...
1482.60 0.38 ACTq L1006 DMA_DIRECT2D Gd<-gates  x1
...
1484.57 2.89 ACTq L958 DMA_DIRECT2D spilled<-res  x1
```

An issue two microseconds behind the gates' load took 2.89 us where others take 0.33. No term of the forecast has it.

- **Ahead of the loop**: 8.2 forecast, 4.95 came. In the 17 traces that have the changed kernel's code ahead of the loop, the loop starts between 1491.5 and 1496.5, so one pair of traces can't tell the two numbers apart. The same rows after:

```profile
1466.80 1.29 DVE L1740 TENSOR_TENSOR ohg<-oh,gpart 128x1024 f16<-128x1024 f16 x2
...
1482.73 0.57 DVE L1762 TENSOR_TENSOR bank<-bank,Gd 128x384 f32<-128x384 f32 x1 [14.64 <-DMA Gd<-gates]
...
1490.15 1.95 PE L2327 MATMUL bank<-cs,xT 128*128 128x128 f32 x16
1491.85 0.71 PE L2379 MATMUL bank<-hi,WH 128*128 128x512 f32 x2
```

In these two traces DVE ends its last batch 1473.12 - 1466.80 = 6.3 us earlier, not 10.5; from there to the first product it takes 25.05 instead of 23.68 us, 1.4 more, where the sum had 1.8 for the turn of x and 0.5 for the weights. Why four batches fewer bring 6.3 was not tried; PE waited 9.4 us for two table remainders of DVE between the batches, 2.5 before.
- **The end**: 7.2 forecast, 6.0 measured. The last two products start at 2436.41, the last two scalings at 2439.11, and the store ends 2.4 us after them.

```profile
2436.41 0.61 PE L2379 MATMUL bank<-hi,WL 128*128 128x512 f32 x2
...
2439.11 1.41 DVE L1803 SCALAR_TENSOR_TENSOR acc<-bank,inverse,gain_row 128x512 f32<-128x512 f32 x2
```

The terms of the miss, each by the run that takes it away, one after the other. The late gathers: 39.8 - 8 = 31.8 us in the first part and 1.5 in the joint part (e6). The held issues on top of that: 5.1 and 11.7 (e9). DVE's long operations in joint turns: 11.4 (e12). The pitch of products: 6.9 (e1). The start and the chain: 2.1 (e9, 15.6 for 13.5). Together 70.5 of the 70.6 us. The order matters: held issues alone give back 21.5 us (e5), since some 5.6 us of the first part are shared. e10 takes the first two away and gains the chain's 0.15 us a turn.

What stays open: why issues behind many small pieces are held for anything from 1 to 10 us, why half clock follows some waits and not others of the same length, and whether the joint part can be brought from 669.5 to 660.3 with six buffers.

## What to carry to other kernels

Price an operation in the place where it will stand: check for each operand whether it moves between PSUM and SBUF, and which engine reads SBUF at that time. A slack computed from a latency is too thin when the op behind the late data can itself be held up, so give gathers all the lead that the buffers allow. Don't put an issue behind a load of many small pieces on the same queue when the engine that issues it has other work.

## What the runs showed of the hardware

- DVE with two operands in SBUF stands still while a POOL instruction that reads SBUF runs, and the other way round: 3.42 instead of 1.22 us for 128x1024, always ending 1.08 to 1.13 us behind POOL's instruction; POOL's remainders end 2.23 to 2.26 us behind DVE's, its slow gathers 0.81 to 0.84. With one operand in PSUM (gating, remainder of weights) no operation of DVE took more than 0.57 us.
- An engine that issues a transfer behind 768 KB in 256 B pieces on its queue is held: up to 9.56 us for one issue on ACT in the changed kernel, up to 9.75 on SP (e15). Behind table tiles of 512 KB in 4 KB pieces SP's issues took 0.45 us at most. Larger pieces for the gates were not tried.
- After a wait of 1.93 us PE was granted 1.2 GHz for about 3 us, two products in 0.86 instead of 0.45 us; eight of the 13 waits in the first part had this behind them, and it cost about a third of what late rows cost.
- Splitting a 1024-column remainder on POOL into four raised it from 2.73 to 4.08 us.
